# A two-layer fp32 decoder trunk on one core: the second unit's weights split ahead of the slabs, and the sum over channels in fp32r

## The chip, the cores and the metric

One core of a Trainium2 chip runs the whole program. The metric is the device time of one execution in microseconds; lower is better.

## The reference

The input `x` is 512 tokens of 1024 channels. Two layers follow one another. Each is a token mixer, an MLP and a gated embedding, all added to the residual `h`, each behind an RMSNorm:

```python
for i in range(DEPTH):                      # 2
    hn = rmsnorm(h, norm_mix[i])
    mix = dilated_mixture_attention(...) if i % 2 == 0 else differential_attention(...)
    h = h + mix                             # both end in @ w_o
    h = h + squared_relu_mlp(rmsnorm(h, norm_mlp[i]), w_ff1[i], w_ff2[i])
    gate = jax.nn.sigmoid(rmsnorm(h, norm_ple[i]) @ w_ple_gate[i])
    h = h + gate * (p[i] @ w_ple_proj[i])
return rmsnorm(h, final_norm)
# rmsnorm(x, g) = x * rsqrt(mean(x*x) + eps) * g
```

All is fp32. The weights come to some 150 MB and are read once.

## The kernel before, in words

**Layout.** Activations lie channels on partitions, tokens in the free dimension: `h` is 8 slabs of 128x512. A projection is cut into *units* of 128 output channels. A unit's weights are 8 blocks of 128x128.

**Three passes.** Each fp32 operand is kept as two fp32r parts, `hi` and `lo` (value minus `hi`). A block is three matmuls over 512 tokens (`passes`, L1647 to L1649): hi x hi, lo x hi, hi x lo. A unit is 24 such passes.

**The pipeline of a unit.** SyncE loads the raw weights of unit `u` into `w_raw[u % 2]` once the split of unit `u - 2` is done (`load`, L675). ScalarE copies them to `w_hi` (`split_hi`, L880) as soon as they have landed and the buffer is free. VectorE subtracts to get `w_lo` (`split_lo`, L1187). TensorE multiplies. VectorE takes the bank (`evac_done`). The units are numbered through: `U_AF` is the first unit of layer 0's MLP, `U_B` the first of the second mixer, `U_BF` the first of layer 1's MLP, `U_AG` and `U_BG` those of the gates. `next_hi(u)` and `next_lo(u)` split unit `u + 1`. Each engine works through its own program in order; a waiting instruction holds all behind it. There is no planner: the order is the order in which the Python code emits for each engine, tied by counting semaphores.

**A norm.** The gain is applied to `h` when a slab is split into `act_hi` and `act_lo` (L895, L1202). The factor `rstd` per token is applied to a unit's *result*, so the units can start before it is known. For it ScalarE squares each slab, GpSimd adds the eight squares into `sumsq` (L862), a matmul with a matrix of ones adds over the channels (`statistics`, L1718, into `attn`), ScalarE takes the root (L913), VectorE the reciprocal (L1207). Until `rstd` is there no unit behind the norm can leave its bank. The first two units use `unit_out0` and `unit_out1`, the third uses `misc`, the fourth needs the second unit's bank again.

**The start of an MLP.** In `out_late` the last one or two slabs of the mixer's output are multiplied by all of `w_o` (the late units). For each of the 8 slabs VectorE adds the result to `h` (L1419), ScalarE writes `act_hi` and the square, VectorE writes `act_lo`, and TensorE does that slab of the MLP's first unit. The first unit's weights lie in a buffer of their own in the idle `qk_hi`; its split stands ahead of the slabs. The second unit (`U_AF + 1`, `U_BF + 1`) is split in the usual buffer behind the last slab. After the first unit TensorE does the sum over channels in plain fp32, then the second unit.

**The gates** (norms 2 and 5) already split `sumsq` into two fp32r parts and sum with two fp32r passes in the middle of their second unit (L1944, L1945).

Of the kernel before, what the change touches and what calls it, by code (L numbers as in the profile page):

```python
# [213 lines left out]

def is_third(u):

    return u.reg is None and u.const in (U_AF + 2, U_B + 2, U_BF + 2)
# [25 lines left out]
def build(nc, x, p, rel_bias, a_w_qkv, a_w_o, b_w_qkv, b_w_o, lq1, lk1, lq2, lk2, subln, norm_mix,  # L243
          norm_mlp, w_ff1, w_ff2, norm_ple, w_gate, w_proj, final_norm, selector, out):
    ctx = ExitStack()
    with ctx:
# [137 lines left out]
        def weights_of(u):  # L384

            if is_start_third(u):
                return [x[0][:, :, :].rearrange("p a (b c) -> p (a b) c", c=P) for x in (ple_hi, ple_lo)]
            if not is_first_up(u):
                return w_hi[u.const % 2], w_lo[u.const % 2]
            first = (0, 14 * T)[u.const == U_BF]  # L390
            both = qk_hi[:, first:first + 2 * KC * P].rearrange("p (n k c) -> p n k c", n=2, c=P)
            return both[:, 0, :, :], both[:, 1, :, :]
# [474 lines left out]
        def _(sc):  # L867
            def split_hi(u, values=None):
# [9 lines left out]
                if not is_first_up(u) and not is_start_third(u):  # L878
# [19 lines left out]
            def slab(w, n, h, dst, written, count):  # L898
# [7 lines left out]
                else:  # L906
                    wait(sc, sumsq_done, w - 1 - KC)
                    sc.activation(square[w % 2][:, :], h[:, n, :], ACT.Square  # L908
                                  ).then_inc(square_ready, 1)

# [53 lines left out]
            def sub_a(s, par, i, has_proj, has_attn):  # L964
# [34 lines left out]
                if has_attn and i == A_UNITS - 1:  # L999
# [3 lines left out]
                                  ).then_inc(o_hi_ready, 1)  # L1003
                if start:
# [22 lines left out]
            def out_late(layer, first, w0, h, dst):  # L1027

                late = LATE[layer]
                if layer:  # L1030
                    for i in range(late):
# [7 lines left out]
            def mlp_of(layer, first, norm, h):  # L1039
                def up(u, k, n, is_first):  # L1040
                    two_ahead = u.reg is None
                    if is_first or not two_ahead:
                        next_hi(u)
                    if two_ahead and n < KC - 1:
# [16 lines left out]
            def gate_of(layer, first, norm, dst):  # L1061
                for n in range(KC):
                    u = At(first + n)
                    if n == 0:
                        next_hi(u)
                        sc.wait_ge(sumsq_done, norm * KC)
                        sc.activation(sumsq_parts[:, 0, :], sumsq[:, :], ACT.Copy).then_inc(sumsq_hi_ready, 1)
# [7 lines left out]
                    sc.activation(scaled[:, :], scaled[:, :], ACT.Sigmoid).then_inc(sigm_ready, 1)  # L1075
                    slab((norm + 1) * KC + n, n, h_b, dst, gated_ready, layer * KC + n + 1)
# [12 lines left out]
            def sub_b(s, par, i, has_proj, has_scores, has_prev, has_norm):  # L1089
# [3 lines left out]
                next_hi(u + i if has_proj else early[0])  # L1093
# [86 lines left out]
        def _(ve):  # L1180
# [18 lines left out]
            def slab_lo(w, n, h, dst):  # L1199
# [3 lines left out]
                                        ALU.mult, ALU.subtract).then_inc(act_ready, 1)  # L1203

# [76 lines left out]
            def sub_a(s, par, i, has_proj, has_attn):  # L1281
# [74 lines left out]
                if has_attn and i == A_UNITS - 1:  # L1356
# [3 lines left out]
                                     ).then_inc(o_ready, 1)  # L1360
                if has_proj and a_values(par, i):
# [47 lines left out]
            def out_late(layer, first, w0, h, dst):  # L1409
# [3 lines left out]
                if layer:  # L1413
                    for i in range(late):
# [17 lines left out]
            def mlp_of(layer, first, norm, h):  # L1432
                def up(u, k, n, is_first):
                    two_ahead = u.reg is None
                    if is_first or not two_ahead:
                        next_lo(u)
                    if two_ahead and n < KC - 1:
# [25 lines left out]
            def gate_of(layer, first, norm, dst):  # L1463

                for n in range(KC):
                    u = At(first + n)
                    if n == 0:
                        next_lo(u)
                        ve.wait_ge(sumsq_hi_ready, layer + 1)
                        ve.tensor_tensor(sumsq_parts[:, 1, :], sumsq[:, :], sumsq_parts[:, 0, :], ALU.subtract  # L1470
                                         ).then_inc(sumsq_lo_ready, 1)
# [32 lines left out]
            def sub_b(s, par, i, has_proj, has_scores, has_prev, has_norm):  # L1504
# [34 lines left out]
                if not opening:  # L1539
# [104 lines left out]
        def _(te):  # L1644
# [290 lines left out]
            def gate_of(layer, first, norm):  # L1935
                for n in range(KC):
# [3 lines left out]
                    if n == 1:  # L1940
                        unit(u, IN[layer], part=(0, 3))
                        te.wait_ge(ones_ready, 1)
                        te.wait_ge(sumsq_lo_ready, layer + 1)
                        te.matmul(attn[:, :], ones_r[:, :], sumsq_parts[:, 0, :], start=True, stop=False)  # L1944
                        te.matmul(attn[:, :], ones_r[:, :], sumsq_parts[:, 1, :], start=False, stop=True  # L1945
                                  ).then_inc(stat_ps, 1)
# [32 lines left out]
            def sub_b(s, par, i, has_proj, has_scores, has_prev, has_norm):  # L1979
# [25 lines left out]
                if has_proj:  # L2005

                    opening = s.reg is None and s.const == 0 and i == 0
                    if turns_head:
# [5 lines left out]
                    if opening:  # L2014
                        statistics(3)
# [94 lines left out]
```

## Time and profile before

| | |
|---|---|
| three runs | 1615.24, 1615.69, 1618.39 us; median 1615.69 |
| profiled execution | 1614.48 us, its span 1612.6 us |
| TensorE | 1598.4 us busy, 99% of the span |
| VectorE | 906.3 us, 56% |
| ScalarE | 607.3 us, 38% |
| GpSimd | 65.9 us, 4% |
| granted TensorE clock | 0.998 of full speed on average |

The span runs from the first to the last instruction; the time holds 1.9 us more around it. Matmuls overlap in the records, so a record of 0.39 us does not mean that TensorE takes a new one only every 0.39 us: the distance between starts tells the pace. "Idle before, releaser" at the end of a row says how long the engine had stood still before it and what ended that.

### The profile page before, as it was taken

The page shows a single profiled execution, that of the slowest core. Times are in us where ns is not written, and L with a number is a line of the kernel's source. Part 1 is how long each engine was busy: PE and PEld are TensorE (multiplying, and loading weights), DVE is VectorE, ACT ScalarE, POOL GpSimd, SP SyncE. Part 2 cuts the span into 40 slices and gives each one's busy share as a digit, 9 for nine tenths or more (in the row PEclk, how much of TensorE's full clock was granted, in tenths as well). Part 3 has the DMA queues.
Part 4 walks back from the last instruction along what each step waited for, and adds up shares of the span by engine and source line. Part 5 has one row for each costly group of instructions (what it writes and reads, how often), then busy time and mean ns, then how long its engine had stood idle before and what let it go on. Part 6 is the DMA issues. An engine that isn't in the chain of part 4 may idle for free.

```text
span 1612.6 us, 22051 instructions
## 1 busy us (share of the span) xinstructions
PE 1598.4 (99%) x8244; PEld 1319.4 (82%) x8244; DVE 906.3 (56%) x1585; ACT 607.3 (38%) x1092; POOL 65.9 (4%) x68
## 2 busy tenths in 40 slices
PE   9999999999999999999999999999999999999998
PEld 7888888888888788888888878888878888888887
DVE  5365464464455863635455676777675363535555
ACT  5234334333333531312223445676652222222344
POOL 1000000000000200000001110000020000000111
PEclk9999999999999999999999999999999999999999
DMA  6633433433322333333333333323233333333331
GB/s 165 161 105 96 127 104 93 120 112 86 101 84 69 105 91 103 93 96 94 97 92 103 98 111 92 92 80 93 62 92 103 93 91 104 91 104 91 92 111 72
DMA packets 300571, 160.12 MB, mean 99 GB/s; under 512 B 31545, under 2 KB 295282, under 8 KB 300514
## 3 DMA queue, kind: packets, MB, share of 16 engines
q1 hardware_dynamic: 300112, 158.61, 34.6%
q0 software_dynamic: 144, 0.71, 0.2%
q8 instruction: 37, 0.61, 0.2%
q14 instruction: 20, 0.16, 0.0%
q10 hardware_dynamic: 258, 0.04, 0.0%
HBM read 157.11 MB, written 10.60 MB: 104 GB/s over the span
## 4 chain that ended last, share of the span: by engine, by line
PE 95%; POOL 1%; DVE 1%; DMA 1%; ACT 1%; issue 0%; SPq 0%; POOLq 0%; ACTq 0%; DVEq 0%
PE unit_out L1647 26%; PE unit_out L1649 26%; PE unit_out L1648 25%; PE turned L1723 2%; PE attn L1792 2%; POOL sumsq L862 1%; PE attn L2037 1%; PE unit_out L1811 1%; PE logits L1723 1%; PE unit_out L1812 1%; PE unit_out L1813 1%; DMA w_raw<-in_a_w_qkv_dram 1%; PE logits L1647 1%; PE misc L1723 1%; PE misc L1647 1%; PE misc L1649 1%
## 5 line engine op out<-in xcount | busy, mean ns | idle before, releaser
L1647 PE MATMUL unit_out<-act_hi,w_hi 128*128 128x512 f32 x1849 | 726.5, 393 | 1.4 <-DVE act_lo L1202 1.0
L1649 PE MATMUL unit_out<-act_hi,w_lo 128*128 128x512 f32 x1849 | 718.7, 389 | 0.0
L1648 PE MATMUL unit_out<-act_lo,w_hi 128*128 128x512 f32 x1849 | 718.0, 388 | 0.0
L880 ACT ACTIVATE w_hi<-w_raw 128x1024 fp32r<-128x1024 f32 (+3 forms) x256 | 271.0, 1058 | 459.4 <-PE unit_out L1649 348.2
L1647 PEld LDWEIGHTS unit_out<-act_hi,w_hi 128*128 128x128 f32 x1849 | 347.2, 188 | 76.3 <-DVE w_lo L1187 2.8
L1649 PEld LDWEIGHTS unit_out<-act_hi,w_lo 128*128 128x128 f32 x1849 | 347.1, 188 | 72.5
L1648 PEld LDWEIGHTS unit_out<-act_lo,w_hi 128*128 128x128 f32 x1849 | 347.5, 188 | 69.7 <-issue 0.2
L1187 DVE TENSOR_TENSOR w_lo<-w_raw,w_hi 128x1024 fp32r<-128x1024 f32 (+3 forms) x256 | 320.2, 1251 | 119.3 <-ACT w_hi L880 119.3
L1049 ACT ACTIVATE act_hi<-hidden 128x512 fp32r<-128x512 f32 x64 | 40.5, 633 | 243.4 <-DVE hidden L1445 243.4
L862 POOL TENSOR_TENSOR sumsq<-sumsq,square 128x512 f32<-128x512 f32 x41 | 57.8, 1410 | 1523.9 <-ACT square L908 1522.2
L1442 DVE TENSOR_TENSOR scaled<-unit_out,rstd 128x512 f32<-128x512 f32 x62 | 42.8, 690 | 67.8 <-PE unit_out L1649 67.7
L1266 DVE TENSOR_TENSOR h_a<-h_a,unit_out 128x512 f32<-128x512 f32 x39 | 26.8, 687 | 90.0 <-PE unit_out L1649 90.0
L1266 DVE TENSOR_TENSOR heads<-heads,unit_out 128x512 f32<-128x512 f32 x40 | 27.5, 686 | 84.2 <-PE unit_out L1649 84.2
L988 ACT ACTIVATE probs<-probs,w_raw 128x256 f32<-128x256 f32 (+1 forms) x128 | 61.7, 483 | 32.4 <-DVE w_raw L1290 32.4
L1448 DVE TENSOR_TENSOR act_lo<-hidden,act_hi 128x512 fp32r<-128x512 f32 x64 | 44.3, 692 | 44.7 <-ACT act_hi L1049 44.7
L1445 DVE SCALAR_TENSOR_TENSOR hidden<-scaled 128x512 f32<-128x512 f32 x64 | 44.3, 692 | 2.2
L1526 DVE CUSTOM_DVE_ANT_0 probs<-logits,bias 128x512 f32<-128x512 f32 (+3 forms) x64 | 28.2, 486 | 26.0 <-PE logits L1649 26.0
L1105 ACT ACTIVATE probs<-probs,low 128x512 f32<-128x512 f32 (+3 forms) x64 | 35.4, 554 | 7.4 <-DVE low L1526 7.4
L895 ACT ACTIVATE act_hi<-heads,gains 128x512 fp32r<-128x512 f32 x24 | 17.3, 722 | 49.1 <-DVE heads L1266 25.6
L1358 DVE TENSOR_TENSOR act_lo<-attn,act_hi 128x512 f32 (+1 forms) x8 | 5.5, 690 | 53.6 <-ACT act_hi L1002 53.6
L1275 DVE TENSOR_SCALAR probs<-probs,w_raw 128x256 f32<-128x256 f32 (+1 forms) x128 | 35.2, 339 | 0.3
L1290 DVE CUSTOM_DVE_ANT_0 probs<-logits,bias 128x256 f32<-128x256 f32 (+1 forms) x64 | 21.1, 386 | 20.4 <-PE logits L1774 20.4
(291 smaller groups left out, 1414.4 us busy)
## 6 DMA issues: line engine op xcount, KB each, us to landing
w_raw<-in_w_ff_dram SPq DMA_DIRECT2D x128, 512.0 KB, 4.0
w_raw<-in_a_w_qkv_dram SPq DMA_DIRECT2D x56, 512.0 KB, 3.9
w_raw<-in_b_w_qkv_dram SPq DMA_DIRECT2D x24, 512.0 KB, 5.1
w_raw<-in_a_w_qkv_dram SPq DMA_DIRECT2D x32, 256.0 KB, 3.0
w_raw<-in_w_ple_gate_dram SPq DMA_DIRECT2D x16, 512.0 KB, 4.1
bias_tiles_b<-bias_vectors SPq DMA_DIRECT2D x16, 256.0 KB, 4.3
bias<-bias_tiles_b SPq DMA_DIRECT2D x8, 512.0 KB, 3.7
w_raw<-in_a_w_o_dram SPq DMA_DIRECT2D x8, 448.0 KB, 3.6
```

The source lines that it names most:

```text
L862: pool.tensor_tensor(sumsq[:, :], sumsq[:, :], square[n % 2][:, :], ALU.add).then_inc(sumsq_done, 1)
L880: sc.activation(weights_of(u)[0][:, 0:width, :], w_raw[par][:, 0:width, :], ACT.Copy).then_inc(hi_done, 1)
L988: e = sc.activation(probs[i][:, cols], probs[i][:, cols], ACT.Exp, bias=low_col, scale=-1.0, accum_out=sum_col)
L1187: ve.tensor_tensor(lo[:, 0:width, :], w_raw[par][:, 0:width, :], hi[:, 0:width, :], ALU.subtract).then_inc(lo_done, 1)
L1266: ve.tensor_tensor(h[:, n, :], h[:, n, :], unit_out[u.const % 2][:, :], ALU.add).then_inc(evac_done, 1)
L1442: ve.tensor_tensor(scaled[:, :], bank_of(u)[:, :], rstd[:, :], ALU.mult).then_inc(evac_done, 1)
L1445: ve.scalar_tensor_tensor(hidden[:, :], scaled[:, :], 0.0, scaled[:, :], ALU.max, ALU.mult).then_inc(hid_ready, 1)
L1448: ve.tensor_tensor(MID[layer][1][:, n, :], hidden[:, :], MID[layer][0][:, n, :], ALU.subtract).then_inc(hid_done, 1)
L1647: te.matmul(bank, w_k[0], hi, start=start, stop=False)
L1648: te.matmul(bank, w_k[0], lo, start=False, stop=False)
L1649: return te.matmul(bank, w_k[1], hi, start=False, stop=stop)
L1723: last = te.transpose(bank[:, dst:dst + P], src, ident[:, :])
```

## The change

Three things change at the norms 1 (before the MLP of layer 0), 3 (before the second mixer) and 4 (before the MLP of layer 1).

The second unit behind the norm is split ahead of the slabs. For the two MLPs it gets a buffer of its own in `qk_hi`, as the first unit has: behind the last attention output of layer 0, and as a third turn of the loop at the head of `out_late` in layer 1. For the second mixer it stays in the usual buffer, and its split is moved into the last step of the gate: on ScalarE behind the sigmoid, on VectorE between the addition and the slab's `act_lo`.

The sum over channels is done as at the gates: ScalarE copies `sumsq` to an fp32r part, VectorE subtracts for the other, and TensorE makes two fp32r passes with `ones_r`. They stand in the middle of the second unit, behind 4 of its 8 blocks.

ScalarE calls a square root on one element ahead of its copy of `sumsq`, which loads the table for the real one.

```diff
@@ weights_of
-            if not is_first_up(u):
+            if not is_first_up(u) and not is_second_up(u):
                 return w_hi[u.const % 2], w_lo[u.const % 2]
-            first = (0, 14 * T)[u.const == U_BF]
+            first = {U_AF: 0, U_AF + 1: 4 * T, U_BF: 14 * T, U_BF + 1: 8 * T}[u.const]
@@ ScalarE, split_hi
-                if not is_first_up(u) and not is_start_third(u):
+                if not is_first_up(u) and not is_second_up(u) and not is_start_third(u):
                     wait(sc, units_done, u - 1)
@@ ScalarE
+            def split_sumsq_hi(norm):
+                if norm != 2 and norm != 5:
+                    sc.activation(spare[:, :], eps_col[:, 0:1], ACT.Sqrt)
+                sc.wait_ge(sumsq_done, norm * KC)
+                sc.activation(sumsq_parts[:, 0, :], sumsq[:, :], ACT.Copy).then_inc(sumsq_hi_ready, 1)
@@ ScalarE, sub_a, last slot (VectorE alike with next_lo)
                                   ).then_inc(o_hi_ready, 1)
+                    if not has_proj:
+                        next_hi(At(U_AF))
@@ ScalarE, out_late (VectorE alike)
                 if layer:
-                    for i in range(late):
+                    for i in range(late + 1):
                         next_hi(At(first + KC + i))
@@ ScalarE, mlp_of up (VectorE alike, with split_sumsq_lo)
-                    if is_first or not two_ahead:
+                    if not two_ahead:
                         next_hi(u)
+                    if is_first:
+                        split_sumsq_hi(norm)
                     if two_ahead and n < KC - 1:
                         next_hi(u + 1)
                     if is_first:
                         statistics(norm)
@@ ScalarE, gate_of
                     sc.activation(scaled[:, :], scaled[:, :], ACT.Sigmoid).then_inc(sigm_ready, 1)
+                    if n == KC - 1:
+                        next_hi(At(U_B))
                     slab(...)
@@ VectorE, gate_of
+                    if layer == 0 and n == KC - 1:
+                        next_lo(At(U_B))
                     if dst is not None:
                         slab_lo((norm + 1) * KC + n, n, h_b, dst)
@@ VectorE
+            def split_sumsq_lo(norm):
+                ve.wait_ge(sumsq_hi_ready, norm)
+                ve.tensor_tensor(sumsq_parts[:, 1, :], sumsq[:, :], sumsq_parts[:, 0, :], ALU.subtract
+                                 ).then_inc(sumsq_lo_ready, 1)
@@ ScalarE, sub_b (VectorE alike, with split_sumsq_lo(3) and next_lo)
+                if s.reg is None and s.const == 0 and i == 0:
+                    split_sumsq_hi(3)
+                else:
+                    next_hi(u + i if has_proj else early[0])
@@ TensorE, statistics
-                te.wait_ge(sumsq_done, norm * KC)
-                te.matmul(attn[:, :], ones[:, :], sumsq[:, :], start=True, stop=True
+                te.wait_ge(ones_ready, 1)
+                te.wait_ge(sumsq_hi_ready, norm)
+                te.matmul(attn[:, :], ones_r[:, :], sumsq_parts[:, 0, :], start=True, stop=False)
+                te.wait_ge(sumsq_lo_ready, norm)
+                te.matmul(attn[:, :], ones_r[:, :], sumsq_parts[:, 1, :], start=False, stop=True
                           ).then_inc(stat_ps, 1)
@@ TensorE, mlp_of up (sub_b alike at its second unit, statistics(3))
-                    if is_first:
+                    if u.reg is None and n == 1:
+                        unit(u, IN[layer], part=(0, 4))
                         statistics(norm)
-                    else:
+                        unit(u, IN[layer], part=(4, KC)).then_inc(units_done, 1)
+                    elif not is_first:
                         whole(u, IN[layer])
```

## Rows read from the trace of the kernel before

**Rows 1.** The page: busy us, share of span; and the splits' ScalarE half.
```profile
PE 1598.4 (99%) x8244; PEld 1319.4 (82%) x8244; DVE 906.3 (56%) x1585; ACT 607.3 (38%) x1092; POOL 65.9 (4%) x68
...
L880 ACT ACTIVATE w_hi<-w_raw 128x1024 fp32r<-128x1024 f32 (+3 forms) x256 | 271.0, 1058 | 459.4 <-PE unit_out L1649 348.2
```

**Rows 2.** Waits of TensorE: who on whom, us in total, times, longest.
```profile
PE unit_out L1647 <- DVE act_lo L1202: 3.5, 7, 0.7
```

**Rows 3.** Order of time, TensorE, first MLP: start, us, engine, line, operation, idle before.
```profile
554.78 0.40 PE L1649 MATMUL unit_out<-act_hi,qk_hi 128*128 128x512 f32 x1
555.34 1.13 PE L1718 MATMUL attn<-sumsq,ones 128*128 128x512 f32 x2 [0.16 <-POOL sumsq L862]
556.43 0.50 PE L1647 MATMUL unit_out<-act_hi,w_hi 128*128 128x512 f32 x1
...
568.35 0.39 PE L1647 MATMUL unit_out<-act_hi,w_hi 128*128 128x512 f32 x1
```

**Rows 4.** The tile sumsq_parts: count, ns min/median/max, first and last start.
```profile
L1067 ACT ACTIVATE sumsq_parts<-sumsq x2: 632/633/634, 903.8 to 1546.9; 128x512 fp32r<-128x512 f32 x2
...
L1945 PE MATMUL attn<-sumsq_parts,ones_r x2: 389/389/389, 909.3 to 1552.3; 128*128 128x512 f32 x2
```

**Rows 5.** Order of time, VectorE, first MLP.
```profile
537.21 1.23 DVE L1187 TENSOR_TENSOR qk_hi<-w_raw,qk_hi 128x1024 fp32r<-128x1024 f32 x1 [0.59 <-ACT qk_hi L880]
...
540.15 1.38 DVE L1419 TENSOR_TENSOR h_a<-h_a,logits 128x512 f32<-128x512 f32 x2 [1.12 <-PE logits L1649]
...
565.96 0.68 DVE L1442 TENSOR_TENSOR scaled<-unit_out,rstd 128x512 f32<-128x512 f32 x1
```

**Rows 6.** Two loads of a second unit's weights: issue, and its us to landing.
```profile
536.84 0.38 SPq L675 DMA_DIRECT2D w_raw<-in_w_ff_dram  x1
DMA to landing us min/median/max: 4.1/4.1/4.1
...
1182.21 0.39 SPq L675 DMA_DIRECT2D w_raw<-in_w_ff_dram  x1
DMA to landing us min/median/max: 4.2/4.2/4.2
```

**Rows 7.** Order of time, VectorE, second MLP.
```profile
1184.38 1.28 DVE L1419 TENSOR_TENSOR heads<-heads,logits 128x512 f32<-128x512 f32 x2
...
1194.61 0.67 DVE L1422 TENSOR_TENSOR heads<-heads,turned 128x512 f32<-128x512 f32 x1
...
1209.88 0.68 DVE L1442 TENSOR_TENSOR scaled<-unit_out,rstd 128x512 f32<-128x512 f32 x1
```

**Rows 8.** Order of time, TensorE, second MLP.
```profile
1184.68 0.39 PE L1649 MATMUL turned<-act_hi,w_lo 128*128 128x512 f32 x1
...
1200.36 0.50 PE L1647 MATMUL unit_out<-act_hi,w_hi 128*128 128x512 f32 x1
...
1205.97 0.39 PE L1647 MATMUL misc<-act_hi,w_hi 128*128 128x512 f32 x1
...
1211.41 0.39 PE L1647 MATMUL unit_out<-act_hi,w_hi 128*128 128x512 f32 x1
```

**Rows 9.** Order of time, VectorE and TensorE, norm before the second mixer.
```profile
960.11 0.75 DVE L1202 SCALAR_TENSOR_TENSOR act_lo<-heads,gains,act_hi 128x512 fp32r<-128x512 f32 x1 [0.79 <-ACT act_hi L895]
...
972.64 0.68 DVE L1197 TENSOR_TENSOR qk_lo_b<-h_a,qk_hi 128x512 fp32r<-128x512 f32 x1
...
974.29 0.50 PE L1647 MATMUL logits<-qk_hi 64*128 64x512 f32 x2
```

**Rows 10.** Order of time, ScalarE: the root at the three norms.
```profile
557.65 0.69 ACT L913 ACTIVATE root<-attn,eps_col 128x512 f32<-128x512 f32 x1
...
964.34 0.69 ACT L913 ACTIVATE root<-attn,eps_col 128x512 f32<-128x512 f32 x1
...
1201.57 0.69 ACT L913 ACTIVATE root<-attn,eps_col 128x512 f32<-128x512 f32 x1
```

**Rows 11.** Stretch after the last matmul: busy us by engine, then granted TensorE clock.
```profile
1607.00:1608.00 1.00, 0.00 (x0) 0.00 (x0) 0.67 (x1) 1.00 (x1) 0.00 (x0) 0.50 1.01 406
```

More of the change, by code:

```diff
@@ L212, in is_first_up, with is_second_up @@
     return u.reg is None and u.const in (U_AF, U_BF)
+def is_second_up(u):
+    return u.reg is None and u.const in (U_AF + 1, U_BF + 1)
 def is_third(u):
@@ L1065, in gate_of @@
                         next_hi(u)
-                        sc.wait_ge(sumsq_done, norm * KC)
-                        sc.activation(sumsq_parts[:, 0, :], sumsq[:, :], ACT.Copy).then_inc(sumsq_hi_ready, 1)
+                        split_sumsq_hi(norm)
                     if n < KC - 1:
@@ L1092, in sub_b @@
                 early = [] if has_proj else b_drain(s, i)
-                next_hi(u + i if has_proj else early[0])
+                if s.reg is None and s.const == 0 and i == 0:
+                    split_sumsq_hi(3)
+                else:
+                    next_hi(u + i if has_proj else early[0])
                 if s.reg is None and s.const == 0 and i == 1:
@@ L1360, in sub_a @@
                                      ).then_inc(o_ready, 1)
+                    if not has_proj:
+                        next_lo(At(U_AF))
                 if has_proj and a_values(par, i):
@@ L1413, in out_late @@
                 if layer:
-                    for i in range(late):
+                    for i in range(late + 1):
                         next_lo(At(first + KC + i))
@@ L1434, in up @@
                     two_ahead = u.reg is None
-                    if is_first or not two_ahead:
+                    if not two_ahead:
                         next_lo(u)
+                    if is_first:
+                        split_sumsq_lo(norm)
                     if two_ahead and n < KC - 1:
@@ L1468, in gate_of @@
                         next_lo(u)
-                        ve.wait_ge(sumsq_hi_ready, layer + 1)
-                        ve.tensor_tensor(sumsq_parts[:, 1, :], sumsq[:, :], sumsq_parts[:, 0, :], ALU.subtract
-                                         ).then_inc(sumsq_lo_ready, 1)
+                        split_sumsq_lo(norm)
                         next_lo(u + 1)
@@ L1538, in sub_b @@
                     out_of(u + (i - 1), B_ORDER[i - 1], par)
-                if not opening:
+                if s.reg is None and s.const == 0 and i == 0:
+                    split_sumsq_lo(3)
+                elif not opening:
                     next_lo(u + i if has_proj else early[0])
@@ L1941, in gate_of @@
                         unit(u, IN[layer], part=(0, 3))
[L1942 to L1946, printed above, removed]
+                        statistics(norm)
                         unit(u, IN[layer], part=(3, KC))
@@ L2007, in sub_b @@
                     opening = s.reg is None and s.const == 0 and i == 0
-                    if turns_head:
+                    if s.reg is None and s.const == 0 and i == 1:
+                        unit(u + i, IN[1], part=(0, 4))
+                        statistics(3)
+                        unit(u + i, IN[1], part=(4, KC)).then_inc(units_done, 1)
+                    elif turns_head:
                         unit(u + i, IN[1], part=(0, KC // 2))
@@ L2013, in sub_b @@
                         whole(u + i, IN[1], act_ready if opening else None, 3 * KC)
-                    if opening:
-                        statistics(3)
                 else:
```

## The prediction

> **What bounds the kernel now.** The page's busy list comes first: TensorE is busy for 99% of the span [rows 1], so the time is what TensorE has to issue plus the few places where it waits. The waits of TensorE come next: the longest entry is `act_lo` on VectorE, 3.5 us in 7 waits [rows 2]. These lie at the norms that the change touches, so the third view is the order of time there, engine by engine.
>
> At the norm before the first MLP, the last pass of its first unit starts at 554.78. The sum over channels follows at 555.34, when GpSimd has finished its additions, takes 1.13 us, and the second unit starts at 556.43 [rows 3]. One pass has a pitch of 0.227 us: from 1205.97 to 1211.41 [rows 8] are 24 passes, one unit. So 556.43 - 554.78 - 0.23 = 1.42 us are lost. A unit that follows a pause also takes longer: 1200.36 to 1205.97 is 5.61 against 5.44, 0.17 more. The other two norms, before the second mixer and the second MLP, show the same pattern; I use the same 1.42 + 0.17 for all three.
>
> Ahead of each MLP, VectorE is the slow engine: per slab an addition and an `act_lo`, gapless from 540.15 until the last `act_lo`, whose end releases TensorE's last slab [rows 2, 5]. The same chain runs from 1184.38 [rows 7]. TensorE ends such a unit when VectorE ends its chain, and whatever delays the start of the chain delays the unit.
>
> **The change, part by part.** *The two passes.* At a gate, the pass of this form that the kernel already has is like any other, 389 ns long [rows 4], so two cost two pitches, 0.45 us, instead of the 1.42 + 0.17. If the second unit follows the first without a pause, this is worth 1.14 us at each of three norms. Bounds: 0.45 more if each pass drained alone (0.39 plus a restart), and nothing below 0.45.
>
> *The second unit's split ahead of the slabs, first MLP.* ScalarE and VectorE take work in program order, so a split that waits for its raw weights holds the slabs behind it. The load of this unit is issued at 536.84 and lands 4.1 us later, at 540.96 [rows 6]. Nothing in the change brings it forward: it waits for the split two units earlier. ScalarE's half lasts 1.06 [rows 1], to about 542.03. VectorE's half is of the form that started at 537.21 and lasts 1.23; instructions of VectorE overlap by 0.09, so its pitch is 1.14. It runs from 542.07, and the first addition, now at 540.15 [rows 5], starts at 543.21: 3.06 later. Behind the waiting split stand all eight slabs, GpSimd's additions of their squares, and TensorE's eight slabs of the first unit. The chain behind has no gap, so I move it whole: +3.06. Bounds: 0, if VectorE could make up 3 us in eight slabs, and 4.2, if its 1.14 came on top, which is in the 3.06 already; the waits of the chain are too few for the first, so the value stays at the whole shift. The split that leaves VectorE's queue behind the last `act_lo` saves nothing more: it lay in the pause already counted.
>
> TensorE then: +3.06 - 1.14 = +1.92 at the third unit. That moves the fourth unit from 568.35 [rows 3] to 570.27. The fourth unit needs the second one's bank, and that waits for `rstd`. The second unit starts at 554.78 + 0.23 + 3.06 = 558.07. Four slabs of it are 12 passes, so the two passes of the sum start at 560.79 and 561.02. The square root may start 0.39 after the last, at 561.41. Now it starts at 557.65 [rows 10], so VectorE's product of the second unit, now at 565.96 and 0.68 long [rows 5], ends at 570.40. Hence a small wait, and a start near 570.5: +2.15 in all. The input of the sum is no limit: GpSimd's end moves with the chain to about 558.35, and the two halves of the split of the sum (the first is 0.63 at the gates [rows 4], the second one product of VectorE, 0.68 [rows 5]) end near 559.8. The early activation that loads the square root's table is hidden in that wait for GpSimd. If it weren't, ScalarE would be 1.3 us later, and still before the two passes.
>
> *The same, second MLP.* The load is issued at 1182.2 and lands 4.2 later, at 1186.4 [rows 6]. Split: ScalarE to 1187.48, VectorE from 1187.52, next instruction at 1188.66 instead of 1184.38 [rows 7]: +4.28. TensorE would reach the fourth unit at 1211.41 + 4.28 - 1.14 = 1214.55. The second unit starts at 1200.36 + 4.28 - 1.42 = 1203.22, the last pass of the sum at 1206.17, the square root at 1206.56 instead of 1201.57 [rows 10]; the second unit's product, now 1209.88 plus 0.68 [rows 7], ends at 1215.55. So the wait for the bank decides: start near 1215.6, +4.2. Without the shift of the slabs the same sum gives 1211.3 against 1211.41: the gain of this junction is eaten by the later sum in any case.
>
> *The norm before the second mixer.* The raw weights have landed long before, so ScalarE's half fits into its pause. VectorE's half sits just ahead of the last `act_lo`, in a pause of 0.79 [rows 9] that ScalarE's `act_hi` ends; its 1.14 from the end of the addition before (about 959.25) reach to 960.39 instead of 960.11: +0.28. The second unit then starts 1.42 - 0.28 earlier, at 962.0, and TensorE is 0.8 ahead. But the root now starts later (962.0 + 13 x 0.227 + 0.39 = 965.3 instead of 964.34 [rows 10], 1.0), and the low half of K, now 972.64 and 0.68 long [rows 9], ends at 974.3. The scores, now at 974.29 [rows 9], wait for it: about 974.4. Net +0.1.
>
> *The rest.* Later loads into the freed raw buffer go out earlier, which nothing waits for; the gates keep their instructions and places and only wait for other counts. Zero, with 0.1 either way.
>
> **Sum.** 2.15 + 0.1 + 4.2 = 6.4 us. The profiled execution has a span of 1612.6 and a time of 1614.48, 1.9 around it; its span becomes 1619.0. The median of the three runs is 1615.69, 1.2 above the profiled one. On it the forecast is 1622.1.
>
> **Rivals.** *A: the slabs do not move.* The split would have to find its weights landed, or VectorE slack in its chain. For it: the addition at 540.15 came after 1.12 us of idle time [rows 5]. Against: the landing times [rows 6], later than the first additions by 0.8 and 2.0 us before any splitting. Then the first MLP's norm gives -1.14 and the other two 0 to +0.1: 1614.6, no difference that can be measured. Chance 0.08.
>
> *B: faster.* The three pauses behind the first units close and nothing opens in their place: 3 x 1.14 = 3.4, 1612.3. It starts to decide once both slab chains move by less than 1.14 and the product of the second unit comes 1 us sooner than worked out above. For it: the pauses are real [rows 3, 8]. Against: the loads again, and that the fourth unit and the scores wait for `rstd`, which the change makes later against TensorE. Chance 0.03.
>
> *C: slower, by the clock too.* Ahead of the second MLP, TensorE now stands still between 1184.68 + 0.23 [rows 8] and the first addition's end, 1189.3: 4.4 us with nothing to issue. Where the kernel's own matmuls end, after thin work, the granted clock goes from 1.00 to 0.50 [rows 11], that is from 2.4 to 1.2 GHz. If it falls in this pause, a pitch of 0.227 becomes 0.454. TensorE then has three groups of 9 passes, 2.04 us each, and 6 passes more before VectorE's last addition can start. At full speed they end near 1197.1, and that addition stands at 1194.61 [rows 7] + 4.28 = 1198.9: 1.8 us of slack. One group and a half at half speed costs 3.1 - 1.8 = 1.3, two groups 2.3, all of it 7.5 - 1.8 = 5.7. I price it at two groups: 1622.1 + 2.3 = 1624.4. Chance 0.25. The Trainium skill ("TensorE: Matmul & The Clock Gate", Part 1) says that the idle state is the throttled one and that activity releases it: by that rule the clock falls here and is back before the unit ends. The trace agrees at its end and has no other pause so long, so the rule speaks for C, against the change.
>
> *D: less than the full price.* The two loads land up to 0.5 us earlier (the landings shown, 4.1 and 4.2, have only two samples), or VectorE closes up a little once its split no longer runs beside GpSimd: +3.5 to +5.5, about 1620.5. Chance 0.12.
>
> **How the numbers follow.** The forecast has 0.52, A 0.08, B 0.03, C 0.25, D 0.12. Its own range is 1620.7 to 1623.5 (0.5 us on either shift, and 0.4 for the spread of the two runs that agree). The 8 in 10 range takes in D and most of C: 1618.9 to 1625.8. A measurement of this kernel tells 0.2%, 3.2 us, from no change. Faster: B, 0.03. Same: A and the low edge of D, 0.11. Slower: the rest, 0.86.
>
> **What would show it.** On ScalarE and VectorE a split into `qk_hi` just ahead of the first slab's addition, waiting for the load; the first addition near 543.2, and at the second MLP near 1191 (1188.66 and the 2.2 us of the stages before). No pause between first and second unit, 12 passes and then the two of the sum. TensorE waiting for VectorE's product at the fourth unit of the second MLP. The granted clock below 1.00 in the second pause decides C. The forecast is wrong if the first addition stands where it stood, or if the chain behind it closes up.

## The result: 0.48% slower, where 0.40% was forecast, and the profile after

| | before | after |
|---|---|---|
| median | 1615.07 us (1614.38 to 1618.39, 6 runs) | 1623.12 us (1621.44 to 1623.95, 6 runs) |
| span of the profiled execution | 1612.6 us | 1621.4 us |
| granted clock, mean | 0.998 | 0.996 |

The ratio is 1.0048, 95% interval [1.0037, 1.0058]. The forecast was 1622.1: 6.4 us on top of a median of 1615.69 over three runs. Over six runs the median before is 1615.07, so the change costs 8.05 us against the 6.4 forecast.

The page after, busy us and share of the span, to set against [rows 1]:

```profile
PE 1599.9 (99%) x8244; PEld 1322.0 (82%) x8244; DVE 906.1 (56%) x1588; ACT 609.8 (38%) x1098; POOL 66.0 (4%) x68
```

TensorE is busy 1.5 us more, the span is 8.8 longer: most of the loss is waiting. (The time holds 1.9 us around the span before and 2.2 after; more on this below the table.) The waits of TensorE name it (us in total, times, longest):

```profile
PE unit_out L1679 <- DVE act_lo L1222: 5.6, 10, 1.0
PE logits L1679 <- DVE heads L1447: 4.4, 1, 4.4
...
PE unit_out L1679 <- DVE scaled L1472: 1.0, 1, 1.0
PE logits L1679 <- DVE qk_lo_b L1217: 0.9, 1, 0.9
```

[Rows 2] had 3.5 us in 7 waits for `act_lo` as their longest entry. Three entries stand beside it now that were not there.

**First MLP.** ScalarE, then VectorE, in order of time (start, us, engine, line, operation, idle before and its releaser):

```profile
541.18 1.06 ACT L885 ACTIVATE qk_hi<-w_raw 128x1024 fp32r<-128x1024 f32 x1 [2.79 <-DMA w_raw<-in_w_ff_dram]
```
```profile
542.27 1.23 DVE L1207 TENSOR_TENSOR qk_hi<-w_raw,qk_hi 128x1024 fp32r<-128x1024 f32 x1 [3.16 <-ACT qk_hi L885]
543.41 1.28 DVE L1447 TENSOR_TENSOR h_a<-h_a,logits 128x512 f32<-128x512 f32 x2
```

These rows show two engines that stand still for 2.79 and 3.16 us behind a load, with all eight slabs queued behind them. The first addition is at 543.41 instead of 540.15 [rows 5]. TensorE at the end of this chain:

```profile
557.43 0.51 PE L1679 MATMUL unit_out<-act_hi,qk_hi 128*128 128x512 f32 x1 [0.72 <-DVE act_lo L1222]
557.78 0.40 PE L1680 MATMUL unit_out<-act_lo,qk_hi 128*128 128x512 f32 x1
558.01 0.40 PE L1681 MATMUL unit_out<-act_hi,qk_hi 128*128 128x512 f32 x1
558.24 0.39 PE L1679 MATMUL unit_out<-act_hi,qk_hi 128*128 128x512 f32 x1
...
560.97 0.39 PE L1751 MATMUL attn<-sumsq_parts,ones_r 128*128 128x512 f32 x1
561.20 0.39 PE L1753 MATMUL attn<-sumsq_parts,ones_r 128*128 128x512 f32 x1
561.42 0.39 PE L1679 MATMUL unit_out<-act_hi,qk_hi 128*128 128x512 f32 x1
...
570.77 0.47 PE L1679 MATMUL unit_out<-act_hi,w_hi 128*128 128x512 f32 x1
```

The second unit follows the first without a pause (558.24 is one pitch behind 558.01), and the sum is two pitches in its middle. What the change aimed at has happened: of the 3.2 us by which the chain came late, some 0.8 are won back. Against 568.35 [rows 3] the fourth unit is 2.42 late.

**Second MLP.** VectorE, and then TensorE:

```profile
1190.12 1.23 DVE L1207 TENSOR_TENSOR qk_hi<-w_raw,qk_hi 128x1024 fp32r<-128x1024 f32 x1 [2.96 <-ACT qk_hi L885]
1191.27 1.28 DVE L1447 TENSOR_TENSOR heads<-heads,logits 128x512 f32<-128x512 f32 x2
...
1200.25 0.69 DVE L1447 TENSOR_TENSOR heads<-heads,turned 128x512 f32<-128x512 f32 x1 [0.40 <-PE turned L1681]
...
1202.36 0.69 DVE L1450 TENSOR_TENSOR heads<-heads,turned 128x512 f32<-128x512 f32 x1 [0.76 <-PE turned L1681]
```
```profile
1192.00 0.80 PE L1679 MATMUL logits<-act_hi,w_hi 128*128 128x512 f32 x1 [4.36 <-DVE heads L1447]
1192.59 0.63 PE L1680 MATMUL logits<-act_lo,w_hi 128*128 128x512 f32 x1
1193.02 0.63 PE L1681 MATMUL logits<-act_hi,w_lo 128*128 128x512 f32 x1
...
1219.84 0.47 PE L1679 MATMUL unit_out<-act_hi,w_hi 128*128 128x512 f32 x1 [1.03 <-DVE scaled L1472]
```

The same wait once more, and TensorE stands still for 4.36 us. Behind that pause a pass lasts 0.63 and its pitch is 0.43 us. The windows of this stretch say why (busy us by engine, then the granted clock, DMA share, GB/s):

```profile
1189.00:1190.00 1.00, 0.00 (x0) 0.00 (x0) 0.00 (x0) 0.96 (x1) 0.00 (x0) 1.00 0.87 254
1190.00:1191.00 1.00, 0.00 (x0) 0.00 (x0) 0.88 (x1) 0.09 (x1) 0.00 (x0) 0.72 0.69 208
...
1194.00:1197.00 3.00, 3.00 (x9) 2.35 (x8) 3.00 (x6) 2.62 (x5) 2.42 (x2) 0.50 0.32 97
1197.00:1198.00 1.00, 1.00 (x6) 0.78 (x5) 1.00 (x2) 0.92 (x2) 0.86 (x2) 0.87 0.00 0
1198.00:1199.00 1.00, 1.00 (x6) 0.83 (x5) 0.96 (x3) 0.42 (x2) 1.00 (x1) 1.00 0.00 0
```

The clock fell from 1.00 to 0.50, 2.4 to 1.2 GHz, while TensorE had nothing to issue. It came back near 1197. TensorE was behind by then, and VectorE, which led the chain before, waits for it (0.40 and 0.76 above). The fourth unit starts 8.43 late against 1211.41 [rows 8].

### The profile page after: what moved, and what is told of

Its sections match the earlier page's. It is cut to its first block, busy times and chain, and to the rows that moved or that the text cites. A ratio compares the mean times of both kernels' runs of the same rounds, so it can differ in the third digit from the quotient of the medians.

```text
span 1621.4 us, 22061 instructions
## 1 busy us (share of the span) xinstructions
PE 1599.9 (99%) x8244; PEld 1322.0 (82%) x8244; DVE 906.1 (56%) x1588; ACT 609.8 (38%) x1098; POOL 66.0 (4%) x68
## 4 chain that ended last, share of the span: by engine, by line
PE 94%; DVE 3%; DMA 1%; ACT 1%; issue 0%; SPq 0%; ACTq 0%; DVEq 0%
PE unit_out L1679 26%; PE unit_out L1681 25%; PE unit_out L1680 25%; PE turned L1758 2%; PE attn L1827 1%; PE attn L2072 1%; PE unit_out L1846 1%; PE logits L1758 1%; DVE act_lo L1222 1%; PE unit_out L1847 1%; PE unit_out L1848 1%; PE logits L1679 1%; DMA w_raw<-in_a_w_qkv_dram 1%; PE misc L1758 1%; DVE rstd L1233 1%; PE logits L1680 1%
## 5 line engine op out<-in xcount | busy, mean ns | idle before, releaser
L1679 PE MATMUL unit_out<-act_hi,w_hi 128*128 128x512 f32 (+1 forms) x1833 | 720.1, 393 | 2.7 <-DVE act_lo L1222 1.3
L1681 PE MATMUL unit_out<-act_hi,w_lo 128*128 128x512 f32 (+1 forms) x1833 | 712.5, 389 | 0.0
L1680 PE MATMUL unit_out<-act_lo,w_hi 128*128 128x512 f32 (+1 forms) x1833 | 711.7, 388 | 0.0
L1207 DVE TENSOR_TENSOR w_lo<-w_raw,w_hi 128x1024 fp32r<-128x1024 f32 (+3 forms) x254 | 315.4, 1242 | 119.7 <-ACT w_hi L885 119.7
```

The costliest lines, as they stand in the source:

```text
L1207: ve.tensor_tensor(lo[:, 0:width, :], w_raw[par][:, 0:width, :], hi[:, 0:width, :], ALU.subtract).then_inc(lo_done, 1)
L1679: te.matmul(bank, w_k[0], hi, start=start, stop=False)
L1680: te.matmul(bank, w_k[0], lo, start=False, stop=False)
L1681: return te.matmul(bank, w_k[1], hi, start=False, stop=stop)
```

## The experiments

A program that runs twice does not reach the first of these norms at the same instant, so I set each profiled execution to zero at the last unchanged instruction ahead of it, VectorE's split at 537.21 in before [rows 5]. That split itself waits for a load; set to the addition before it (534.25 in before) the first column moves by less than 0.15, but in e4 it is then -0.5 instead of -0.2. This table is the key to all that follows: us by which each norm makes TensorE later than before, at the fourth unit of the first MLP, at the scores of the second mixer, at the fourth unit of the second MLP.

| | first MLP | mixer | second MLP | sum | median over before |
|---|---|---|---|---|---|
| forecast | 2.15 | 0.1 | 4.2 | 6.4 | 6.4 |
| after | 2.4 | 0.2 | 5.8 | 8.4 | 8.05 |
| e2, split alone | 2.9 | -0.1 | 3.9 | 6.8 | 6.7 |
| e1, sum alone | 2.3 | 1.5 | 1.8 | 5.7 | 5.1 |
| e9, e1 once more | 0.7 | 1.6 | 3.1 | 5.4 | 5.55 |
| e7, e1 and passes in one pause | 0.8 | 1.5 | 1.8 | 4.1 | 5.3 |
| e8, e1 and passes in three pauses | 0.8 | 1.5 | 1.7 | 4.0 | 4.4 |
| e3, after and passes in the 4.4-us pause | 2.3 | 0.1 | 4.2 | 6.6 | 7.2 |
| e4, raw weights early | -0.2 | 0.2 | 1.1 | 1.1 | 0.8 |
| e6, split among the slabs | 1.1 | 0.2 | 2.6 | 3.9 | 4.8 |
| e5, e4 and two reorderings | -0.7 | -0.7 | -0.8 | -2.1 | -2.4 |

The first four columns come from one execution each, the last from medians. Two things lie in no column of the norms. The time outside the span is 1.9 us in every execution of before and of e2 (1.87 to 1.97) and 2.1 to 2.3 in all kernels with the new sum: 0.3 us of their medians come with the new sum and lie outside what the profile shows. Why was not tested. And in after the clock fell at 1613.7, ahead of the last matmuls of the final norm:

```profile
1613.70 0.57 PE L2109 MATMUL unit_out<-ones,square 128*128 128x1 f32 x2
```

In before the same row stands at 1605.19 and lasts 0.36, and the clock falls at 1606.2, when the last matmul (1605.86, 0.41 long) is almost done. That is where the span of after gains the 0.4 us by which its 8.8 exceed the table's 8.4; in e3, where the clock fell behind the last matmul, nothing is added after the third norm.

**e1: the sum alone.** The splits of the second units are back behind the last slab and in the usual buffer.

```diff
 def is_second_up(u):
-    return u.reg is None and u.const in (U_AF + 1, U_BF + 1)
+    return False
...
-                    for i in range(late + 1):
+                    for i in range(late):
                         next_hi(At(first + KC + i))
...
```

> The change's sum (two fp32r passes in the middle of the second unit) without its early splits: the second unit is split behind the slabs again, in the usual buffer. Theory Q (the loss of the change is the split that waits at the head of the slabs' queue, plus the clock): no slab chain moves. The second unit of each MLP starts where it did, since VectorE's split beside GpSimd ended only then; the sum now comes 12 passes later, so rstd is 2 us later: about +0.5 us at the first MLP, +1.9 at the second mixer, +1.3 at the second MLP, 3.7 in all, near 1618.8 against 1615.1. Granted clock 1.00 in the second MLP. Rival S (the later sum is what makes the change slow): most of the change's 8 us, 1621 or more. Rival P (the cheaper sum pays by itself): 1.1 us less at each of three norms, 1611.8.

Measured: 1620.25 us (1619.73 to 1623.76), ratio 1.0036 [1.0024, 1.0048]. That is 1.4 more than I expected. So each part of the change loses by itself, and the two losses (5.1 here, 6.7 in e2) do not add up to the 8.05 of both. TensorE at the first MLP:

```profile
556.33 0.50 PE L1670 MATMUL unit_out<-act_hi,w_hi 128*128 128x512 f32 x1 [1.26 <-DVE w_lo L1202]
556.66 0.45 PE L1671 MATMUL unit_out<-act_lo,w_hi 128*128 128x512 f32 x1
556.91 0.63 PE L1672 MATMUL unit_out<-act_hi,w_lo 128*128 128x512 f32 x1
...
560.76 0.39 PE L1742 MATMUL attn<-sumsq_parts,ones_r 128*128 128x512 f32 x1
```

and the granted clock there:

```profile
556.00:557.00 1.00, 0.67 (x3) 0.58 (x4) 1.00 (x3) 0.80 (x1) 0.00 (x0) 0.93 0.00 0
557.00:558.00 1.00, 1.00 (x4) 0.81 (x3) 1.00 (x1) 0.00 (x0) 0.00 (x0) 0.50 0.29 63
```

Two things follow. The pause between the first and the second unit stays, 1.26 us, for the split of the second unit's weights (VectorE, 2.30 us long beside GpSimd) fills it as well as the fp32 sum did. The trace of before has that split too, from 554.08 to 556.37, as the first of the two in this row, and TensorE's second unit at 556.43 [rows 3]:

```profile
554.08 3.52 DVE L1187 TENSOR_TENSOR w_lo<-w_raw,w_hi 128x1024 fp32r<-128x1024 f32 x2
```

So the sum was free where it stood, and moving it only makes `rstd` later. And the clock can fall behind a pause of 1.26 us, not only behind one of 4.4.

**e2: the split alone.** The sum is the fp32 matmul again and stands before the second unit.

```diff
-                        unit(u, IN[layer], part=(0, 4))
                         statistics(norm)
-                        unit(u, IN[layer], part=(4, KC)).then_inc(units_done, 1)
+                        whole(u, IN[layer])
...
```

> The change's early splits with the old sum: one fp32 matmul ahead of the second unit, no parts of sumsq. Theory Q: the slab chains move by 3.1 and 4.3 us as in the changed kernel, the old sum moves with them, and the clock falls in the same pause: +3.1 at the first MLP, 0 at the second mixer, +5.9 at the second MLP, 9.0 in all: near 1624. Rival S (the later sum is what costs): near the kernel before, 1615 to 1617.

Measured: 1621.79 us (1620.76 to 1622.44), ratio 1.0042 [1.0028, 1.0055]. The rival by which the split is harmless is out: alone it gives 6.7 of the 8.05 us. At the second MLP, TensorE:

```profile
1191.62 0.50 PE L1681 MATMUL logits<-act_hi,w_hi 128*128 128x512 f32 x1 [4.25 <-DVE heads L1449]
1191.96 0.40 PE L1682 MATMUL logits<-act_lo,w_hi 128*128 128x512 f32 x1
```

The pause is about as long as in after (4.25 against 4.36), but the clock was still up at its end; it was 0.66 on average from 1192 to 1197. That cost nothing here: VectorE's last addition comes 9.50 us after this restart, as it does in e3 below with the clock up (9.49). My 1624 was too high by the clock that I had put into it.

**e3: TensorE kept busy in the pause.** Eighteen passes of a matrix of ones by a block of the hidden activations stand ahead of the slabs of the second MLP. Their result is not used.

```diff
+                else:
+                    for i in range(18):
+                        te.matmul(attn[:, :], ones_r[:, :], MID[layer][0][:, 0, :], start=True, stop=True)
                 for n in range(KC):
```

> The changed kernel, with 18 extra fp32r passes of 128x512 (4.1 us, into an idle bank, results unused) in TensorE's pause ahead of the second MLP. If the fall of the clock to 0.50 costs what I read from the trace: the granted clock stays at 1.00, VectorE's additions of slabs 6 and 7 no longer wait for TensorE, the first unit ends 1.6 us sooner: near 1621.5 against 1623.1 of the changed kernel. Rival (the slack of VectorE's chain hides the slow passes): no difference from the changed kernel, 1623.1.

Measured: 1622.33 us (1621.24 to 1622.98), ratio 1.0043 [1.0030, 1.0057]. TensorE and the windows, to set against those of after:

```profile
1188.13 4.24 PE L1740 MATMUL attn<-act_hi,ones_r 128*128 128x512 f32 x18
...
1218.87 0.47 PE L1679 MATMUL unit_out<-act_hi,w_hi 128*128 128x512 f32 x1 [1.03 <-DVE scaled L1472]
```
```profile
1190.00:1191.00 1.00, 1.00 (x6) 0.84 (x5) 0.37 (x1) 0.60 (x1) 0.00 (x0) 1.00 1.07 324
...
1194.00:1197.00 3.00, 3.00 (x14) 2.38 (x14) 3.00 (x5) 3.00 (x6) 1.91 (x2) 1.00 0.48 144
```

The clock stays at 1.00, and this norm costs 4.2 instead of 5.8. So the clock's share is 1.6 us in the profiled execution of after. In the medians it is 0.8, inside their spread: after has executions of 1621.4 and 1621.6 too, and e3 one of 1623.0. The median alone would not show it.

Where the 1.6 us go can be read on VectorE, first in e3, then in after:

```profile
1202.00 0.67 DVE L1450 TENSOR_TENSOR heads<-heads,turned 128x512 f32<-128x512 f32 x1
1202.60 2.87 DVE L1222 SCALAR_TENSOR_TENSOR act_lo<-heads,gains,act_hi 128x512 fp32r<-128x512 f32 x2
```
```profile
1202.96 3.46 DVE L1222 SCALAR_TENSOR_TENSOR act_lo<-heads,gains,act_hi 128x512 fp32r<-128x512 f32 x2
```

TensorE starts again at 1192.51 in e3 and at 1192.00 in after. Counted from there, the last addition comes 0.87 later in after (1202.36 above). The last two `act_lo`, which end the chain, then take 3.46 instead of 2.87, for the first of them now lies beside more of GpSimd's additions (1.77 instead of 1.17). Together 1.5 of the 1.6 us.

**e4: the raw weights early.** The second unit's raw weights get 4 KB per partition of their own in `heads`, which is idle by then, and are loaded at 524.78 and 1174.40, 12 and 8 us sooner. The splits stand where the change puts them.

```diff
+            sp.wait_ge(pv_done, A_PAIRS - 1)
+            load_own(U_AF, 0)
...
+            sp.wait_ge(pv_done, A_PAIRS + B_HEADS * B_ITEMS - 1)
+            load_own(U_BF, 1)
...
```

> The changed kernel, but the second unit's raw weights of both MLPs go to an idle place of their own (no wait for w_raw) and are loaded well ahead of the split; same splits at the same places in the queues. Theory Q: nothing waits at the head of the slabs. The chains then move only by what does not fit into VectorE's idle time: +0.35 us at the first MLP, +1.14 at the second; no long pause, clock 1.00. Sum: -0.6 (first MLP), +0.1 (mixer), +1.1 (second MLP): 0.6, near 1615.7, no difference from before. Rival S: still 1621 or more. Rival P2 (it is the split's own length on the busy engine, not the wait for the load): at least +2.3 at the two chains beyond the changed sums, 1618 to 1620.

Measured: 1615.88 us (1615.36 to 1616.27, 11 runs), ratio 1.0004 [0.9995, 1.0013]. VectorE at the first MLP:

```profile
539.49 1.23 DVE L1239 TENSOR_TENSOR qk_hi<-heads,qk_hi 128x1024 fp32r<-128x1024 f32 x1 [0.25 <-ACT qk_hi L917]
540.63 1.28 DVE L1479 TENSOR_TENSOR h_a<-h_a,logits 128x512 f32<-128x512 f32 x2
```

This decides it. Same order of the splits, same instructions on the engines, no wait for the load: 7.3 us of the 8.05 are gone. At the first MLP the split nearly fits into the 1.12 us for which VectorE waited for TensorE before [rows 5], and the first addition moves from 540.15 to 540.63 only. At the second MLP, where VectorE had no such wait, it costs its own length, the 1.1 us of the table.

**e6: the split among the slabs.** The change, with the second unit's split behind slab 3 (ScalarE) and slab 4 (VectorE), when the late load has landed.

```diff
-                    for i in range(late + 1):
+                    for i in range(late):
                         next_lo(At(first + KC + i))
...
+                    if n == 4:
+                        next_lo(At(first + KC + late))
...
```

> The change with one thing moved: the MLPs' second unit is split in the loop over the slabs, ScalarE behind slab 3 and VectorE behind slab 4, where the raw weights have landed, in the same buffers of their own. The first additions stand where they stood before. Theory (the loss is the wait for the load at the head of the queue, and what VectorE's own split costs is its length): no pause of TensorE over 3 us, granted clock 1.00 in both MLP norms; the chain of VectorE is longer by its split, 1.14, up to 2.3 where it runs beside GpSimd, minus the 1.14 us that the closed pause gives; the later rstd costs some 1 us at the second MLP. About +2 against before, 1616 to 1618, 1617.0 most likely. Rival (any split in the chain ahead of the last slab costs as much as the change does, by order and not by the load): 1621 or more. Second rival (the gain of the closed pause shows in full): 1613.

Measured: 1619.73 us (1617.33 to 1620.71), ratio 1.0028 [1.0015, 1.0040]. More than I expected, less than the change. VectorE at the first MLP:

```profile
546.41 0.67 DVE L1445 TENSOR_TENSOR h_a<-h_a,logits 128x512 f32<-128x512 f32 x1
547.01 1.19 DVE L1222 SCALAR_TENSOR_TENSOR act_lo<-h_a,gains,act_hi 128x512 fp32r<-128x512 f32 x1
548.12 2.31 DVE L1207 TENSOR_TENSOR qk_hi<-w_raw,qk_hi 128x1024 fp32r<-128x1024 f32 x1
```

The split lasts 2.31 us beside GpSimd's additions instead of 1.23. Minus the closed pause that is the 1.1 us of the table. The second MLP costs 2.6; there the clock was 0.50 again, from about 1200.1 to 1203.5, in the gaps behind the slabs. No run separates that from what the later `rstd` costs at this place. The one of the six executions with a mean clock of 0.998 took 1617.33, the expected time; the others, at 0.996 and 0.997, took 1619.6 and more.

The Trainium skill ("GPSIMD Engine Reference", Specifications) says that GpSimd shares its interfaces to the on-chip memory with VectorE and gets in the way of instructions that read two tensors there. The rows agree: the split and `act_lo` read two (1.23 becomes 2.31, 0.75 becomes 1.19), the addition reads one of its two from TensorE's bank and stays at 0.67.

**e5: a version that beats both.** e4, and in layer 1 the split whose weights came first goes first. The sum stands behind 3 of the 8 blocks instead of 4.

```diff
-                    for i in range(late + 1):
+                    for i in (0, 2, 1):
                         next_lo(At(first + KC + i))
...
-                        unit(u, IN[layer], part=(0, 4))
+                        unit(u, IN[layer], part=(0, 3))
...
```

> e4_raw_early with two more edits: at the second MLP the second unit's split goes ahead of the first unit's late block of work (its raw weights are there first), and at the three norms the two passes of the sum stand behind 3 of the 8 blocks instead of 4. Theory (the rest of the loss in e4 is the later rstd, and 1.14 us of split at the head of the second MLP's chain): the sum is 3 passes, 0.68 us, earlier at each norm; at the first MLP the fourth unit is bound by the bank no more than 0.1, about -0.8 against before; at the mixer the scores wait for rstd, -0.55; at the second MLP the first addition stands again within 0.3 of before, and the fourth unit's wait (1.03 in e4) shrinks to 0.3 or less, -0.75. Together -2.1 against before, where e4 has +0.5 in the trace: 1613.0 beside before's 1615.1. Rival (the order of the two splits and the place of the sum cost elsewhere what they give, e.g. the sum's input, the low half of the split of the sum, is late for it and TensorE waits): 1615 to 1616, a wait of TensorE for the parts of the sum in the trace.

Measured: 1612.57 us (1612.27 to 1614.31, 11 runs) beside 1614.97 of before, ratio 0.9987 [0.9978, 0.9996]: faster, by a small amount that the interval keeps apart from none. VectorE at the second MLP:

```profile
1179.53 1.23 DVE L1241 TENSOR_TENSOR w_lo<-w_raw,w_hi 128x1024 fp32r<-128x1024 f32 x1 [0.47 <-ACT w_hi L918]
1180.67 1.22 DVE L1241 TENSOR_TENSOR qk_hi<-heads,qk_hi 128x1024 fp32r<-128x1024 f32 x1
1181.80 1.22 DVE L1241 TENSOR_TENSOR qk_hi<-w_raw,qk_hi 128x1024 fp32r<-128x1024 f32 x1
1182.94 1.28 DVE L1481 TENSOR_TENSOR heads<-heads,logits 128x512 f32<-128x512 f32 x2
```

Three splits without a gap; in e4 VectorE stood still for 1.17 us in their midst. The first addition is at 1182.94 instead of 1184.38 [rows 7], 0.1 sooner than the 1.3 us gained ahead of it. TensorE waits 0.35 instead of 1.03 for the product of the second unit:

```profile
1209.35 0.47 PE L1713 MATMUL unit_out<-act_hi,w_hi 128*128 128x512 f32 x1 [0.35 <-DVE scaled L1506]
```

**e7, e8, e9: is e1's excess the clock?** e7 is e1 with five extra passes in the 1.26-us pause of the first MLP, e8 has them in all three pauses, e9 is e1 once more beside e8. The passes' results are not used. The cut is from e8; e7 has the loop for layer 0 alone.

```diff
                     if u.reg is None and n == 1:
+                        for i in range(5):
+                            te.matmul(attn[:, :], ones_r[:, :], MID[layer][0][:, 0, :], start=True, stop=True)
                         unit(u, IN[layer], part=(0, 4))
...
```

> e1_sum_only with five more fp32r passes of TensorE (a matrix of ones by a block of the hidden activations, result unused) between the first and the second unit at the first MLP alone, where e1 has its 1.26-us pause. Theory (the excess of e1 at that norm is the clock, which fell to 0.50 from 556.9 to 560): the pause is filled with 1.14 us of work, the granted clock stays at 1.00, the sum's passes come at 559.2, the root at 559.8 and the fourth unit at about 568.7 instead of 570.6; time 1618.4 beside e1's 1620.25. Rival (the excess is the order, the wait for w_lo and the later rstd): nothing changes, 1620.2 to 1621. A third way: the clock falls all the same, since the thin stretch ahead of the pause decides and not the pause: 1620.5.

Measured: 1620.29 us (1618.88 to 1621.19), ratio 1.0032 [1.0020, 1.0044]. The trace follows the clock theory: fourth unit at 569.03, span 1616.7 instead of 1618.2. The median does not move, so by itself this run would have decided nothing.

> e7_sum_awake with the five extra passes of TensorE (results unused) in all three 1.26-us pauses of e1_sum_only, not only in the first. In e7 the trace followed the clock theory (fourth unit 1.5 us sooner than in e1, span 1616.7 beside 1618.2), the median did not (1620.29). Theory (the clock can fall behind any of the three pauses, and in some executions does at the later ones): with all three filled the clock stays up, mean 0.998, the median comes to the span of e7's profiled run and about 2 around it, 1618.7, and the spread of the runs shrinks. Rival (the clock behind these pauses has nothing to do with the median): 1620.3 as before. The extra passes themselves cost 0 to 0.1 each pause.

> e1_sum_only once more, beside e8_sum_awake_all on the same chip. Clock theory: 1620.3 again, 1.5 or more above e8_sum_awake_all, with a mean clock of 0.997. Rival: within 0.4 of it.

Measured: e8 1619.06 us (1618.33 to 1620.01, 11 runs), ratio 1.0025 [1.0016, 1.0034]; e9 1620.24 (1619.05 to 1621.37), ratio 1.0031 [1.0019, 1.0043]. e9 repeats e1's median, and e8 is 1.2 below it, against 1.5 expected. The intervals of the ratios overlap, but ten of e8's 11 executions lie under 1619.6 and five of e9's six above 1620.0. In e9's profiled execution the clock held at the first MLP and fell at the second, near 1202.5, at the end of a pause of the same length:

```profile
1202.71 0.80 PE L1670 MATMUL unit_out<-act_hi,w_hi 128*128 128x512 f32 x1 [1.26 <-DVE w_lo L1202]
1203.31 0.63 PE L1671 MATMUL unit_out<-act_lo,w_hi 128*128 128x512 f32 x1
```

That would explain e7, in which two executions took 1618.9 and four 1620.2 or more: with one pause of three filled, the clock can still fall at the others. The table shows it as 2.3 and 1.8 in e1 against 0.7 and 3.1 in e9. The Trainium skill ("TensorE: Matmul & The Clock Gate", Part 1) says of the clock's release at a kernel's start that its point varies from run to run. These two executions of one program show the like for the fall. What is left of e8, 4.0 us (0.8, 1.5 and 1.7 at the three norms), I put down to the later `rstd`: the splits stand where they stood before and the clock is up. The medians add the 0.3 us outside the span.

## Why the prediction was right, point by point

**The first step, the wait for the load**, held. First MLP: first addition forecast 543.21, measured 543.41, and the fourth unit at 570.77 where about 570.5 was forecast; 2.15 became 2.4. Second MLP: forecast +4.28, measured 1191.27 - 1184.38 [rows 7] - 2.60 of the stages before = 4.29. e4 shows that the wait is the loss and not the split's own length. I had moved the whole chain without a gap, and that is what it did.

**The two passes** held. They stand at 560.97 and 561.20, 560.79 and 561.02 forecast. e2 beside after shows a thing that the sum did not say in one place: at the first MLP the fp32r sum gives back 0.5 (2.9 against 2.4), at the mixer it costs 0.3, and over all three norms it comes to about nothing (6.8 in e2, 6.6 in e3, neither with a loss by the clock there). Outside the span the new sum costs the 0.3 us named above, for which my sum had no term. The three closed pauses are paid for by the later `rstd`.

**The mixer** held: +0.1 forecast, +0.2 measured, with a wait of the scores for the low half of K of 0.92 us. The path there is the forecast one, root at 967.85 - 2.42 = 965.4 against 965.3.

**The second MLP** was mis-sized. The step said +4.2, the fourth unit waiting for the second one's product, which is what the trace shows (1.03). It measured 5.8. The missing 1.6 us are rival C, which came true in the profiled execution and which I gave 0.25: e3, with the clock held up, gives the 4.2. C's own price of 2.3, two groups of passes at half speed (4.1) minus VectorE's slack (1.8), was too high by 0.7. The slack was right: TensorE worked at half speed from 1192.0 to 1197.1, which loses 2.5, and VectorE's last addition came 0.87 late, so the slack took 1.7. Wrong were the length of the slow stretch, and that I had no term for the `act_lo` that then ran longer beside GpSimd, 0.6. The median, 1623.12, lies between the forecast and C's 1624.4.

**How much of it is luck.** The forecast of the time, 1622.1, is 1.0 below the measured median; that of the difference, 6.4, is 1.65 short. The base of three runs was 0.6 too high, and that hid a part. The missing time is in terms that stood at nothing: the clock in some executions, 0.3 outside the span, 0.4 at the end of the profiled one. With the clock held up at the second MLP (e3), the three norms cost 6.6, close to the 6.4. In rival D a reading is off as well: +3.5 to +5.5 on 1615.69 is 1620.2 in the middle and not 1620.5; nothing hangs on it.

**What I had not seen.** I took the 1.42 us behind each first unit for the price of the fp32 sum. I had the split in that pause too, "in the pause already counted", but not that it fills it alone: e1 removes the sum and the pause is 1.26 still. The forecast did not suffer, for the change removes both. The rest, +0.4 us, lies behind the third norm, where I put 0 with 0.1 either way: it is the fall of the clock at 1613.7, ahead of the last matmuls.

## What to carry to other kernels

Before an instruction that needs a load is moved ahead of others on an in-order engine, work out when it will be done and compare that with the start of the first instruction behind it. The price, once per place, is landing time plus the work that waits for it minus that start: at the first MLP 540.96 + 2.2 (both halves of the split) - 540.15, about 3.1. The landing alone was only 0.8 late. An earlier load into 4 KB per partition more took the loss here from 8.05 to 0.8 us. A pause that two things fill closes only when both are gone, and doing the free one elsewhere costs what depends on it. Where TensorE pauses, read the granted clock window by window and in more than one execution; a median over a few runs mixes those in which it fell with those in which it held.

## What the runs showed of the hardware that was not expected

The clock fell to 0.50 at the end of a pause of only 1.26 us or just behind it (e1 at 556.9, e9 near 1202.5). Both times TensorE had been waiting for VectorE slab by slab in the microseconds before. In before the same stretch at the first MLP has 1.42 us without passes, the fp32 sum in them, and the clock stayed at 1.00 there. One fall cost 1.5 us in e1 and 1.4 in e9, against e8 at the same norm. In e6 it fell with no pause over 1.5 us. In the profiled executions of e7 and e8 it held in the pauses that five unneeded passes (1.3 us) filled; it held at the first MLP of e9 without them as well, so it is e8's median beside e9's that speaks for the passes. A fall need not cost anything: in e2 the clock was at 0.50 from about 1192.5 to 1195.9 and the chain on VectorE did not wait. What exactly makes it fall at one of the places and not at another stays open.
